# One core of Trainium2: the first pair of up tiles in ordinary form behind the norm, the seven-product sums of x made meanwhile, and the loads at the turn to the down products in another order

## The reference

```python
h2 = rmsnorm(x, g_ffn[i])
u = causal_dwconv(h2 @ w_up[i], conv_w[i], conv_b[i])      # D_FF = 2816, 3 taps
x = x + (jax.nn.gelu(u[..., :D_FF], approximate=True) * u[..., D_FF:]) @ w_down[i]
```

## Time and profile before

| | |
|---|---|
| median of 3 timed runs | 4010.72 us (4006.64 to 4012.73) |
| the profiled execution | 3992.99 us |
| its span, first to last instruction | 3991.2 us |
| TensorE busy | 3675.6 us, 92% of the span |
| VectorE, GpSimd, ScalarE busy | 2023.3, 1874.7, 1214.1 us |
| mean granted TensorE clock | 0.966 |

### The profile page before, as it was taken

How to read it: one execution, slowest core, us unless ns; L and a number is a source line. 1 busy time by engine, 2 the same in 40 slices (tenths; PEclk the granted TensorE clock), 3 DMA queues, 4 the chain that set the end, 5 groups by cost and what they waited for, 6 DMA issues and landing times. The chain is left out here.

```text
span 3991.2 us, 61576 instructions
## 1 busy us (share of the span) xinstructions
PE 3675.6 (92%) x26066; PEld 2786.1 (70%) x26066; DVE 2023.3 (51%) x2298; ACT 1214.1 (30%) x1740; POOL 1874.7 (47%) x1067
## 2 busy tenths in 40 slices
PE   6999899889999899988999997788989799998998
PEld 5888544678778543777776776675577588877877
DVE  4442676552542565633549304435542788873242
ACT  3123344431213344411245212224401344431020
POOL 1332266542333366533346434412633699973433
PEclk9999899999999999999999999998999899999999
DMA  4011200034112100032211210020043122234211
GB/s 183 32 41 65 64 1 1 26 137 170 58 32 72 29 1 1 26 142 65 85 56 47 100 68 4 4 96 1 1 129 114 43 92 83 80 110 140 77 48 69
DMA packets 101960, 258.57 MB, mean 65 GB/s; under 512 B 29232, under 2 KB 38576, under 8 KB 100800
## 3 DMA queue, kind: packets, MB, share of 16 engines
q1 hardware_dynamic: 82864, 215.03, 15.6%
q10 hardware_dynamic: 18832, 39.72, 3.0%
HBM read 200.16 MB, written 54.56 MB: 64 GB/s over the span
## 5 line engine op out<-in xcount | busy, mean ns | idle before, releaser
L1816 PE MATMUL acc<-h_hi,weights_hi 128*128 128x512 f32 (+1 forms) x928 | 364.2, 392 | 7.9 <-DVE h_lo L1977 5.5
L1063 DVE TENSOR_REDUCE part_max<-aux 128x1 f32<-128x428 f32 (+5 forms) x468 | 253.1, 582 | 179.3 <-PE aux L904 127.6
L1818 PE MATMUL acc<-h_hi,weights_lo 128*128 128x512 f32 (+1 forms) x928 | 339.3, 366 | 0.0
L1817 PE MATMUL acc<-h_lo,weights_hi 128*128 128x512 f32 (+1 forms) x928 | 338.6, 365 | 0.0
L2507 PE MATMUL acc<-h_hi,weights_hi 128*128 128x512 f32 x672 | 273.9, 408 | 13.5 <-DVE h_lo L2788 6.8
L1855 POOL TENSOR_TENSOR weights_hi<-weights,ones 128x1024 fp32r<-128x1024 f32 x42 | 80.4, 1914 | 429.7 <-PE acc L1818 389.6
L1991 DVE RECIPROCAL arena<-arena 128x512 f32<-128x512 f32 (+1 forms) x48 | 141.7, 2953 | 260.6 <-ACT arena L1954 260.6
L2509 PE MATMUL acc<-h_hi,weights_lo 128*128 128x512 f32 x672 | 263.4, 392 | 0.0
L2508 PE MATMUL acc<-h_lo,weights_hi 128*128 128x512 f32 x672 | 263.0, 391 | 0.0
L1025 ACT ACTIVATE probs<-acc 128x1024 f32<-128x1024 f32 (+1 forms) x168 | 168.4, 1003 | 254.5 <-PE acc L939 253.8
L3658 PE MATMUL acc<-operand_hi,weights_hi 128*128 128x512 f32 x528 | 211.1, 400 | 25.0 <-DVE operand_lo L3487 20.8
(11 more groups left out here) (501 smaller groups left out, 9129.5 us busy)
## 6 DMA issues: line engine op xcount, KB each, us to landing
weights<-in_w_in SPq DMA_DIRECT2D x44, 512.0 KB, 3.5
arena<-in_w_mod SPq DMA_DIRECT2D x6, 2048.0 KB, 8.8
weights<-in_w_out SPq DMA_DIRECT2D x22, 512.0 KB, 4.8
weights<-in_w_up SPq DMA_DIRECT2D x22, 512.0 KB, 4.8
xT<-in_w_up SPq DMA_DIRECT2D x22, 512.0 KB, 5.0
feed_forward_spill<-xT SPq DMA_DIRECT2D x22, 512.0 KB, 2.9
weight_sums<-feed_forward_spill SPq DMA_DIRECT2D x22, 512.0 KB, 4.6
weights<-in_w_mod SPq DMA_DIRECT2D x4, 2048.0 KB, 26.5
```

The costliest lines, as they stand in the source:

```text
L1063: nc.vector.tensor_reduce(part_max[:, b % 2, j, hh, i:i + 1], max_tile(m)[:, hh, 0:cw], AX_X, ALU.max, negate=True).then_inc(max_done, 1)
L1816: nc.tensor.matmul(out, w_hi[:, b, k, :], hi[:, k, cols], start=(k == 0), stop=False)
L1817: nc.tensor.matmul(out, w_hi[:, b, k, :], lo[:, k, cols], start=False, stop=False)
L1818: return nc.tensor.matmul(out, w_lo[:, b, k, :], hi[:, k, cols], start=False, stop=(k == KD - 1))
```

## The change

- The first pair of tiles is made in ordinary form: 8 k tiles x 4 quarters x 3 passes = 96 matmuls, into four PSUM banks, as the k tiles of x become ready. Its weights are rounded and parted whole, two tiles of 128x1024 (`f_hi`, `f_lo`).
- `SevenNorm` scales x in place, a 128x1024 tile at a time, with the reciprocal norm read from PSUM; ScalarE's copy to `held` is gone. High and low parts of the tiles are the operands' B blocks. The low part is made by VectorE for even k and by GpSimd for odd k.
- The four sums T1 to T4 are made behind that, each by one VectorE operation of 128x2048, with one rounding (ScalarE) and one low part (VectorE) each. T4 lies in `kept_sum`, in tiles of x.
- The other 21 pairs are made with seven products. The ordinary pair's results are copied from PSUM by ScalarE. The convolution of pair i+1's tile follows the products numbered i.
- Buffers in x are laid out anew (`raws`, `raw`, `u`), and `more` has two tiles.
- 22 filler products in place of 40.
- At the turn SyncE loads the first down weights and two g tiles ahead of the store of the last tile but one, the weights of job 2 ahead of the last store, and the tiles of x between the jobs' weights.

```diff
@@ class SevenWeights: high
         if i:
             act.wait_ge(self.made, SEVEN * (i - 1) + o + 1)
+        elif o >= self.n_clear:
+            act.wait_ge(self.first_made, 2)
@@ class SevenNorm
     def scalar(self, act):
+        for k in range(KD):
+            act.wait_ge(self.scaled, k + 1)
+            self.pg.nc.scalar.copy(self.halves(self.hi, k), self.tile(k)).then_inc(self.rounded, 1)
+    def round_sum(self, act, i):
+        o = self.sums[i]
+        act.wait_ge(self.added, self.added_as[RIGHT[o]])
+        if i == 3:
+            act.wait_ge(self.first_made, 2)
+        self.pg.nc.scalar.copy(self.hi[:, o], self.kept_sum if i == 3 else self.whole[:, o]).then_inc(self.sum_rounded, 1)
+    def gpsimd(self, pool):
+        for k in range(1, KD, 2):
+            pool.wait_ge(self.rounded, k + 1)
+            self.pg.nc.gpsimd.tensor_tensor(self.halves(self.lo, k), self.tile(k), full(self.halves(self.hi, k)), ALU.subtract).then_inc(self.odd_parted, 1)
+    def vector(self, dve):
+        dve.wait_ge(self.spread, 2)
+        for k in range(KD):
+            tile = self.x[:, k, :]
+            nc.vector.scalar_tensor_tensor(tile, tile, self.gain(k), flat(pg.aux[:]), ALU.mult, ALU.mult).then_inc(self.scaled, 1)
+            if k % 2:
+                dve.wait_ge(self.rounded, k)
+                nc.vector.tensor_tensor(self.halves(self.lo, k - 1), self.tile(k - 1), full(self.halves(self.hi, k - 1)), ALU.subtract).then_inc(self.even_parted, 1)
+    def sums_by_vector(self, dve):
+        dve.wait_ge(self.scaled, KD)
+        tt(t1, b12, b11, ALU.subtract).then_inc(self.added, 1)
+        dve.wait_ge(self.added, 1)
+        tt(t2, b22, t1, ALU.subtract).then_inc(self.added, 1)
+        tt(t3, b22, b12, ALU.subtract).then_inc(self.added, 1)
+        dve.wait_ge(self.added, 3)
+        dve.wait_ge(self.odd_parted, HALF // 2)
+        tt(self.kept_sum, b21, t2, ALU.subtract).then_inc(self.added, 1)
+        dve.wait_ge(self.added, 4)
+        for i in range(3):
+            self.part_sum(dve, i)
@@ feed_forward, sync
-                for i in range(n_up - 1):
-                    if i + 2 < n_up:
+                for i in range(n_up - 2):
+                    if i + 2 < n_pairs:
                         sp.wait_ge(w.parted, SEVEN * (i + 1))
-                        w.fetch(sp, i + 2, up_tiles(i + 2))
+                        w.fetch(sp, i + 2, up_tiles(i + 3))
                     store(i)
-                sp.wait_ge(w.parted, SEVEN * (n_up - 1))
+                sp.wait_ge(w.parted, SEVEN * n_pairs)
                 down_weights(0)
                 down_weights(1)
-                for t in range(7):
+                fetch_g(0)
+                fetch_g(1)
+                store(n_up - 2)
+                for t in range(2, 7):
                     fetch_g(t)
-                    if t == 1:
-                        fetch_x(0)
-                        fetch_x(HALF)
-                store(final)
-                sp.wait_ge(conv_done, 4 * n_up)
-                for k in (1, 2, 3):
-                    fetch_x(k)
-                for t in (final - 1, final):
-                    sp.wait_ge(g_stored[t % 2], 16 * (t // 2 + 1))
-                for k in (5, 6, 7):
-                    fetch_x(k)
+                fetch_x(0)
+                fetch_x(1)
+                down_weights(2)
+                store(n_up - 1)
                 fetch_g(7)
                 fetch_g(8)
-                for q in range(2, len(jobs)):
+                fetch_x(2)
+                fetch_x(3)
+                down_weights(3)
+                sp.wait_ge(conv_done, 4 * n_up)
+                for q in range(4, len(jobs)):
+                    if q < KD:
+                        fetch_x(q)
...
@@ feed_forward, tensor
                 maker.tensor(pe)
-                keep_busy(pg, pg.acc[:, 0], 40)
-                pe.wait_ge(w.parted, SEVEN)
-                pe.wait_ge(maker.kept, 2)
-                for j in range(HALF):
...
-                for i in range(1, n_up):
+                keep_busy(pg, pg.acc[:, 0], 22)
+                pe.wait_ge(first_parted, 2)
+                for k in range(KD):
+                    maker.ready(pe, k)
+                    for b in range(2):
+                        for c in range(2):
+                            out, hi, lo = first_banks[b][c], maker.half(operand_hi, k, c), maker.half(operand_lo, k, c)
+                            nc.tensor.matmul(out, f_hi[:, b, k, :], hi, start=(k == 0), stop=False)
+                            nc.tensor.matmul(out, f_hi[:, b, k, :], lo, start=False, stop=False)
+                            mm = nc.tensor.matmul(out, f_lo[:, b, k, :], hi, start=False, stop=(k == KD - 1))
+                        if k == KD - 1:
+                            mm.then_inc(first_made, 1)
+                for i in range(n_pairs):
@@ feed_forward, scalar
-                for o in range(SEVEN):
-                    w.high(act, 0, o)
+                for b in range(2):
+                    act.wait_ge(first_loaded[b], 16)
+                    nc.scalar.copy(f_hi[:, b], raw_w[:, b]).then_inc(first_rounded, 1)
                 maker.scalar(act)
+                w.high(act, 0, 0)
+                maker.round_sum(act, 0)
+                w.high(act, 0, 1)
+                w.high(act, 0, 2)
+                maker.round_sum(act, 1)
+                maker.round_sum(act, 2)
+                act.wait_ge(first_made, 2)
+                act.wait_ge(maker.added, 4)
+                for b in range(2):
+                    for c in range(2):
+                        copied = nc.scalar.copy(raw[b][:, 2 + c * BANK:2 + (c + 1) * BANK], first_banks[b][c])
+                    copied.then_inc(first_copied, 1)
+                    w.high(act, 0, 3 + b)
+                maker.round_sum(act, 3)
...
@@ feed_forward, vector
+                maker.part_sum(dve, 3)
+                convolve(0)
+                for i in range(n_pairs):
```

More of the change, by code:

```diff
@@ L3422, with __init__, halves, half @@
 class SevenNorm:
-    def __init__(self, pg, cn, x, operands, gain, second, rstd_all):
-        self.pg, self.cn, self.x, self.gain, self.second, self.rstd_all = pg, cn, x, gain, second, rstd_all
+    def __init__(self, pg, cn, x, operands, gain, kept_sum, first_made):
+        self.pg, self.cn, self.x, self.gain, self.kept_sum, self.first_made = pg, cn, x, gain, kept_sum, first_made
         self.hi, self.lo, self.whole = operands
[L3427 to L3432, removed]
+        self.spread, self.scaled, self.rounded = pg.sem("x_spread"), pg.sem("x_scaled"), pg.sem("x_rounded")
+        self.even_parted, self.odd_parted = pg.sem("even_parted"), pg.sem("odd_parted")
+        self.added, self.sum_rounded, self.sum_parted = pg.sem("x_sums"), pg.sem("sums_rounded"), pg.sem("sums_parted")
+        self.sums = [RIGHT.index(name) for name in ("T2", "T1", "T3", "T4")]
+        self.added_as = {"T1": 1, "T2": 2, "T3": 3, "T4": 4}
+    def halves(self, part, k):
+        first = slice(0, SEVEN, SEVEN - 1) if k < HALF else slice(2, 6, 3)
+        return part[:, first, k % HALF, :]
+    def half(self, part, k, c):
+        o = ((0, SEVEN - 1) if k < HALF else (2, 5))[c]
+        return part[:, o, k % HALF, :]
+    def tile(self, k):
+        return self.x[:, k, :].rearrange("p (c n) -> p c n", c=2)
     def tensor(self, pe):
@@ L3440, in tensor, with ready @@
             mm.then_inc(self.spread, 1)
-    def ready(self, pe, j, o):
-        if o in self.by_dve:
-            pe.wait_ge(self.dve_parted, len(self.by_dve) * j + self.by_dve.index(o) + 1)
+    def ready(self, pe, k):
+        if k % 2:
+            pe.wait_ge(self.odd_parted, k // 2 + 1)
         else:
-            pe.wait_ge(self.pool_parted, len(self.by_pool) * j + self.by_pool.index(o) + 1)
+            pe.wait_ge(self.even_parted, k // 2 + 1)
     def scalar(self, act):
-        nc, pg = self.pg.nc, self.pg
-        for c in range(2):
-            act.wait_ge(self.spread, c + 1)
-            nc.scalar.copy(self.rstd_all[:, c * BANK:(c + 1) * BANK], pg.aux[:, c, :]).then_inc(self.kept, 1)
-        for j in range(HALF):
[L3454 to L3487, removed]
@@ new lines, in part_sum @@
+    def part_sum(self, dve, i):
+        o = self.sums[i]
+        dve.wait_ge(self.sum_rounded, i + 1)
+        self.pg.nc.vector.tensor_tensor(self.lo[:, o], self.kept_sum if i == 3 else self.whole[:, o], full(self.hi[:, o]), ALU.subtract).then_inc(self.sum_parted, 1)
+    def sums_by_vector(self, dve):
+        tt = self.pg.nc.vector.tensor_tensor
+        b11, b12 = (self.x[:, 0:HALF, c * BANK:(c + 1) * BANK] for c in range(2))
+        b21, b22 = (self.x[:, HALF:KD, c * BANK:(c + 1) * BANK] for c in range(2))
+        t2, t1, t3 = (self.whole[:, o] for o in self.sums[:3])
+        dve.wait_ge(self.scaled, KD)
[9 more added lines that the diff above has]
+            self.part_sum(dve, i)
@@ L3601, in _ @@
             def _(sp):
-                w.fetch(sp, 0, up_tiles(0))
-                sp.wait_ge(maker.scaled, 4)
```

(17 more changed lines are left out.)

112 lines of the change are left out of this document (61 added, 51 removed).

## The result

Four timed executions of each (three of the four of before are those that the prediction had): before 4008.68 us (4002.88 to 4012.73), changed 3956.02 us (3955.17 to 3957.22), ratio 0.987, interval 0.9853 to 0.9887, which is 45 to 59 us less. I had written 3969, 3957 to 3988: faster, as forecast, but 1 us outside the range, and 52.7 us won instead of 41.5.

The account below looks back on a forecast made before the run. TensorE was taken to fill the middle, leaving only the start and the turn to win: 3993.0 - 23.5 - 18.0 = 3951.5 us profiled. With the timed runs' 17.7 us carried over, the forecast was 3969 us, range 3957 to 3988.

Parts of the forecast that it names:

- the last of the sum: Whole kernel: the timed median's 17.7 us above the profiled execution carried over, 4010.7 - 41.5 = 3969.2 us.
- The gain of 41.5 us: Feed-forward stage: 23.5 us less at its start and 18.0 us less at the turn to the down products.
- The start, 23.5 us: First pairs of the feed-forward stage: tile pair 2 starts at about 3175 instead of 3198.5, 23.5 us less.
- TensorE alone sets the start: Rival at the start: TensorE's work alone sets the pace, 34 us won there, 52 in all, 3959 us; chance 0.10.
- The first convolution's block: Rival at the start: VectorE held up twice by 7.92 us blocks, 10 us won instead of 23.5, 3983 us; chance 0.14.
- the rule's sum: Start: by the skill's port rule no 7.92 us block comes, so the start gains the summed 23.5 us.
- The turn, 18.0 us: Turn to the down products: 6.5 us from earlier loads plus 11.5 us at the third job.
- The whole chain is paced by loads into two stages, so all of it moves: Turn: first down weights and g tiles issued earlier, so the seventh g tile is ready 6.5 us sooner.
- The third job's term: Down products, third job: weights wait and slow restart gone, 9.2 + 2.7 - 0.4 = 11.5 us less.
- the turn gives back: Rival at the turn: third job waits as long for other things, 6.5 us there, 30 in all, 3981; chance 0.11.
- The middle: Seven-product pairs between start and turn: TensorE-bound at 19.04 us per pair, 20 pairs without gaps, no further gain.
- GpSimd's period: Rival in the middle: GpSimd becomes the bound, 20.64 us per pair costs 32 us, 4002 us; chance 0.10.

Follow-up runs that it names:

- the two later comparisons: Changed kernel timed again, unedited, beside the kernel before: medians 3960.81 and 3960.06 us, ratios 0.990 and 0.991.
- Runs 7 to 9: Changed kernel with the scalings' norm copied to SBUF; with three low parts reading PSUM; with 40 fillers instead of 22: stage 711.87, 700.33, 704.6 us.
- run 2: Kernel before with only SyncE's order at the turn changed: median 3984.05 us, ratio 0.9953, stage 728.81 us.
- run 3: Changed kernel with SyncE's old order at the turn: median 3981.64 us, ratio 0.9947, stage 720.08 us.
- Runs 10 and 12: Changed kernel with six buffers for the first g tiles, the second also rounding tile 6 before the tap: stage 702.18, 697.90 us; medians 3966.52, 3950.38 us.
- run 5: Kernel before with the RWKV scan left out: median 3715.95 us, stage 744.0 us.
- run 7: Changed kernel with the norm copied from PSUM to SBUF by ScalarE before the scalings: stage 711.87 us.

## Why the prediction was wrong, step by step

**The step that failed is the last of the sum**: "The three timed runs have their median at 4010.72, 17.7 us above it; I carry the difference". I took 4010.7 for the level of the session, for the changed kernel too, and 3 us for the spread of its executions. The changed kernel did not carry the 17.7 us: its 3956.02 is 4.5 us above the 3951.5 that the sum gives from the profiled execution, and over 16 executions its median is 3957.9, 6.4 us above. The kernel before shows the same: 48 executions beside the later runs have a median of 3999.2, 6.3 us above the profiled 3992.99, and spread from 3984.5 to 4020.3. With 6.3 in place of 17.7 the sum gives 3957.8.

The gain of 41.5 us was sized well. From the stage's begin to the end of the span it is 39.0 to 41.4 us over the profiles of the two kernels (36.5 in the one pair without the scan), 40.7 by the medians without the scan, 37.4 and 38.2 in the two later comparisons. So the 52.7 of the first comparison is some 12 us too large, and mostly on the side of the kernel before: 4008.7 against 3999.2 later, where the changed kernel has 3956.0 against 3957.9.

That its four executions were only high draws is argued, not shown. Of the 48 others 17 took as long as the lowest of these four or longer, so four in a row would come up about once in 60 comparisons ((17/48)^4 = 0.016). The later comparisons ran on four chips with medians of 3998.2, 3998.8, 3998.2 and 4001.8 for the kernel before; the chip of the first is not on record.

What the executions of one kernel differ by can be read from their mean granted clock, which is on record for each: over the 48 it goes from 0.957 (4015.90 us) to 0.968 (3984.49 us), 3.1 us more for each thousandth less, with a correlation of -0.93. The scan's share is seen in its last stretch (278.1 to 297.7 us); the stages ahead of the feed-forward stage without it differ by 11 us over twelve profiles. Not settled: why the clock differs from execution to execution, and why the first four of the changed kernel lay within 2 us.

**The start, 23.5 us: 23.3 measured.** First matmul at 10.46 by the sum, 10.56 in the trace. That is in part luck: the sum left out the first of ScalarE's two roundings, 1.06 us, and the rounding began 0.94 us earlier than it assumed (3.72 us behind the stage's begin instead of 4.66). The ordinary pair ran without a wait between its matmuls. GpSimd's fifth operation, near 39.8 by the sum, lands at 41.9, and the next pair's first low part, 64.6 by the sum, at 64.91. Left out at this place was the slow restart behind the wait of 9.39 us, 2.7 us: TensorE was through with the seven-product pair at 63.8 and not near 59, so only 1.2 us were left between it and GpSimd. Runs 7 to 9 show the cause: with the scalings' norm in SBUF VectorE needs 5.2 us more, with three operations out of the turns GpSimd is 6.2 us earlier, and a TensorE 3 us later loses nothing. "TensorE alone sets the start" is refuted.

**The first convolution's block.** It came again in the changed kernel, one pair later, and cost nothing:

```profile
3180.71 7.88 DVE L3850 SCALAR_TENSOR_TENSOR xT<-xT,conv_w 128x1024 f32<-128x1024 f32 x1 [1.11 <-ACT xT L3776]
```

The Trainium skill ("SBUF — State Buffer", Who interferes with whom) has the second to issue wait until the first finishes; this one waited while several GpSimd operations passed in a row, in both kernels, and the measurement decides. None came in the stretch that sets the start, so the rule's sum and mine agree.

**The turn, 18.0 us: 16.1 in the stretch, 15.0 to 15.7 in the stage by run 2.** Here the sum was 2 to 3 us too large. The seventh g tile came 13.15 us behind the up products' end, 17.52 before: 4.4 us, not 6.5. "The whole chain is paced by loads into two stages, so all of it moves" left out VectorE's convolution. The g loads did go out 6.9 us earlier (15.8 us ahead of the up products' end, 8.9 before), and the first tiles were rounded in time, but VectorE was still in its convolution, now slowed by GpSimd's down weights, which come beside it since they were loaded earlier:

```profile
3547.76 2.71 DVE L3852 SCALAR_TENSOR_TENSOR more<-xT,conv_w,more 128x1024 f32<-128x1024 f32 x1
3550.51 3.04 DVE L3855 TENSOR_TENSOR more<-more 128x1024 f32<-128x1024 f32 x1
3553.47 0.67 DVE L3537 TENSOR_TENSOR held<-held,acc 128x512 f32<-128x512 f32 x1
3554.07 5.16 DVE L3838 TENSOR_TENSOR operand_lo<-weight_sums,operand_hi 128x1024 fp32r<-128x1024 f32 x2
```

The last two operations of that convolution took 1.28 and 1.22 us before. This is read from the rows; no run moves the convolution alone. Runs 10 and 12 show that the two buffers bind as well, since the third tile's load waits for the first tile's low part: with six buffers and the seventh tile rounded first, the stage is 6 to 8 us shorter. The third job's term, 11.5 us (with 9.2 for a wait of 9.04), comes to 11.7 as the rest of the stretch (16.1 less 4.4), with no wait for VectorE in that profile; "the turn gives back" is refuted.

**The middle.** Twenty pairs in 380.8 us, no wait but the 1.17 us ahead of the first. GpSimd's period did not bind.

Unforeseen: the last stage is 1.2 us shorter in the changed kernel (137.2 to 136.0), which by luck makes up for half of what the turn fell short. It goes with the turn and not with the start: run 2 has 136.0 and run 3 has 137.0, though the kernel before without the scan has 136.2. The place is the 20 us behind that last stage's first 10, where the granted clock was 0.83 in the kernel before and in run 3, and 0.91 in the changed kernel, in run 2 and in run 5. Why, I leave open.

## What to carry to other kernels

Judge a change by the stage it touches, between two marks that both kernels have: here that gave 36.5 to 41.4 us from single profiles, while medians of four to eighteen executions gave 37 to 53. Look at the mean granted clock of each execution before you take a median for a level. A forecast of an absolute time needs the level of many executions; where one profile and the median lie 18 us apart, that distance is itself the spread and belongs in the range. And where two engines take turns, as VectorE and GpSimd do here when VectorE has both inputs in SBUF, add up their operations as one queue, also at the place where a reordering lets them meet for the first time.

## What the runs showed of the hardware

- VectorE with one input in PSUM kept its 1.27 us per 128x1024 beside GpSimd (eight scalings, 1267 to 1281 ns); with both inputs in SBUF the same scalings took 1.27 to 3.45 us, 2.33 in the median (run 7). Of the eight 128x2048 operations of the start, beside GpSimd too, six took 3.3 to 3.4 us, one 4.4 and one 2.3, and GpSimd's 128x512 took 3.2 to 3.35.
- The turns are not always kept: one VectorE operation of 1.28 us took 7.92 us before and 7.88 in the changed kernel.
- After a wait of 9.39 us TensorE's granted clock was 0.52 for 5.5 us; the pair took 21.8 us instead of 19.04.
- The granted TensorE clock in the last eighth of the scan was 1.00, 0.90, 0.74 and 0.54 in four executions of the same code, and the scan took 280.3, 282.9, 289.8 and 296.6 us.
- Over 48 executions of one kernel a mean granted clock lower by 0.001 went with 3.1 us more of some 4000.
